# Attention half of a hybrid block: the right half of an output projection by Strassen-Winograd products, with weight sums kept in HBM and a five-slot weight ring

## The reference

```python
def hybrid_layer(x, norm_g, w_in, b_f, conv_w, w_att_o, w_conv_o, w_out):   # x: 256 tokens x 2048
    h = rmsnorm(x, norm_g)
    q, k, v, f_logit, z_att, u, gate_b, gate_c, z_conv, m_att, m_conv = split(h @ w_in)
    o_att = forgetting_attention(heads(q), heads(k), heads(v), log_sigmoid(f_logit + b_f))
    y_att = (o_att * silu(z_att)) @ w_att_o          # 2048 x 2048, the product that the change touches
    o_conv = gate_b * short_conv(gate_c * u, conv_w)
    y_conv = (o_conv * silu(z_conv)) @ w_conv_o
    merged = sigmoid(m_att) * y_att + sigmoid(m_conv) * y_conv
    return x + merged @ w_out                         # then a final rmsnorm
```

## Time and profile before

| | |
|---|---|
| median of 3 runs | 1208.87 us |
| profiled execution, its own time | 1209.7 us |
| its span, first to last instruction | 1207.9 us |
| TensorE busy | 99% |
| VectorE busy | 77% |
| ScalarE busy | 54% |
| HBM traffic | 231 GB/s over the span |

### The profile page before, as it was taken

How to read it: one execution, slowest core, us unless ns; L and a number is a source line. 1 busy time by engine, 2 the same in 40 slices (tenths; PEclk the granted TensorE clock), 3 DMA queues, 4 the chain that set the end, 5 groups by cost and what they waited for, 6 DMA issues and landing times.

```text
span 1207.9 us, 18425 instructions
## 1 busy us (share of the span) xinstructions
PE 1196.3 (99%) x7252; PEld 1070.2 (89%) x7252; DVE 925.3 (77%) x1095; ACT 651.9 (54%) x868; POOL 35.2 (3%) x50
## 2 busy tenths in 40 slices
PE   9999999999999999999999999999999999999997
PEld 8998898898888988889888899999999999888886
DVE  6989988988989989999966556767676667655544
ACT  7666555556656566656555445445544554543533
POOL 1000000000000000000000010111011101000000
PEclk9999999999999999999999999999999999999999
DMA  6788898898888898898678866556655655665663
GB/s 214 240 294 278 270 297 262 274 300 260 272 289 291 270 292 287 270 309 272 192 238 266 269 184 180 155 180 176 188 155 177 181 170 169 223 207 177 212 227 118
DMA packets 181249, 280.40 MB, mean 232 GB/s; under 512 B 9296, under 2 KB 128160, under 8 KB 180768
## 3 DMA queue, kind: packets, MB, share of 16 engines
q1 hardware_dynamic: 171760, 263.49, 68.3%
q10 hardware_dynamic: 9408, 15.78, 4.2%
HBM read 270.83 MB, written 8.41 MB: 231 GB/s over the span
## 4 chain that ended last, share of the span: by engine, by line
PE 87%; DVE 10%; issue 1%; ACT 1%; DMA 0%; ACTq 0%; POOLq 0%; POOL 0%; DVEq 0%
PE ps L1478 22%; PE ps L1480 22%; PE ps L1479 22%; PE ps L1494 7%; PE ps L1493 6%; PE ps L1495 3%; PE ps L1492 3%; DVE w_lo L1052 2%; DVE w_lo L1089 2%; DVE w_lo L1086 2%; DVE quads L1068 1%; DVE quads L1070 1%; DVE quads L1066 1%; DMA chan_rows<-in_norm_gain 0%; PE ps L1503 0%
## 5 line engine op out<-in xcount | busy, mean ns | idle before, releaser
L934 DVE TENSOR_TENSOR w_lo<-w_raw,w_hi 128x1024 fp32r<-128x1024 f32 x196 | 238.8, 1236 | 99.6 <-ACT w_hi L610 98.9
L1478 PE MATMUL ps<-h,w_hi 128*128 128x258 f32 (+1 forms) x1024 | 293.6, 287 | 1.4 <-DVE w_lo L1052 1.2
L1479 PE MATMUL ps<-h,w_hi 128*128 128x258 f32 (+1 forms) x1024 | 291.2, 284 | 0.0
L1480 PE MATMUL ps<-h,w_lo 128*128 128x258 f32 (+1 forms) x1024 | 290.9, 284 | 0.0
L610 ACT CAST w_hi<-w_raw 128x1024 fp32r<-128x1024 f32 x198 | 204.3, 1051 | 120.1 <-PE ps L1480 74.8
L1478 PEld LDWEIGHTS ps<-h,w_hi 128*128 128x128 f32 x1024 | 192.7, 188 | 5.4 <-issue 1.8
L1479 PEld LDWEIGHTS ps<-h,w_hi 128*128 128x128 f32 x1024 | 192.9, 188 | 2.1
L1480 PEld LDWEIGHTS ps<-h,w_lo 128*128 128x128 f32 x1024 | 192.8, 188 | 0.0
L1052 DVE TENSOR_TENSOR w_lo<-w_raw,w_hi 128x1024 fp32r<-128x1024 f32 x122 | 148.7, 1220 | 15.9 <-ACT w_hi L666 15.7
L1494 PE MATMUL ps<-h,w_hi 128*128 128x512 f32 x408 | 159.9, 397 | 1.0 <-DVE w_lo L1052 0.9
L666 ACT CAST w_hi<-w_raw 128x1024 fp32r<-128x1024 f32 x122 | 127.0, 1049 | 29.2 <-PE ps L1480 25.1
(11 more groups left out here) (211 smaller groups left out, 2055.2 us busy)
## 6 DMA issues: line engine op xcount, KB each, us to landing
w_raw<-in_w_in SPq DMA_DIRECT2D x226, 512.0 KB, 4.9
quads<-in_w_in SPq DMA_DIRECT2D x144, 512.0 KB, 4.5
w_raw<-in_w_conv_o SPq DMA_DIRECT2D x32, 512.0 KB, 5.7
w_raw<-in_w_att_o SPq DMA_DIRECT2D x32, 512.0 KB, 4.6
w_raw<-in_w_out SPq DMA_DIRECT2D x32, 512.0 KB, 4.5
quads<-in_w_in SPq DMA_DIRECT2D x48, 256.0 KB, 5.0
gates_dram<-stage ACTq DMA_DIRECT2D x24, 256.0 KB, 4.9
gate_nat<-gates_dram ACTq DMA_DIRECT2D x8, 512.0 KB, 4.1
```

Of the source, the lines that this page charges most:

```text
L934: nc.vector.tensor_tensor(w_lo[:, lo_slot(c), :], w_raw[:, c % RAW, :], w_hi[:, hi_slot(c), :].bitcast(F32), ALU.subtract).then_inc(w_spli ...
L1478: nc.tensor.matmul(dst, a_hi, b_hi, start=start, stop=False, skip_group_check=resumed)
L1479: nc.tensor.matmul(dst, a_hi, b_lo, start=False, stop=False, skip_group_check=resumed)
L1480: return nc.tensor.matmul(dst, a_lo, b_hi, start=False, stop=stop, skip_group_check=resumed)
```

## The change

Columns 0 to 1023 of `w_att_o` are still multiplied by `natural`-like units (two blocks, `"n"`). For columns 1024 to 2047 the product of 256 tokens x 2048 by 2048 x 1024 is cut in 2 x 2 parts (two token halves, even and odd k tiles, two column halves) and made from seven products of half size in place of eight: 56 products instead of 64. The weight sums T1 to T4 are made by VectorE during the pairs of att, from weights loaded for that purpose (`load_t`, 1 MB a pair), and stored to HBM (`store_t`, `t_dram`, 1 MB a pair); the sums of the attention output, S1 to S4, are made in `finish_pair`, split, stored for seven pairs (512 KB each) and brought back in one 3.5 MB transfer on POOL's queue when wa begins. In wa, sums are loaded back as weight units. Such a unit (`"a"`, `"t1"`, `"b"`, `"t2"`, `"b22"`) is 512 KB as well, but gives two products and not four. Wa has 44 units where it had 32:

```diff
 def hi_slot(c):
-    return (c - U_F) % CONV_RING if c < U_F else (c + 5) % RING
+    return (c - U_WIDE) % CONV_RING if c < U_WIDE else (c - U_WIDE + CONV_RING) % RING
 def slot_reused(c):
-    return RING + c - (CONV_RING if c < U_F else RING) + 1
+    return RING + c - (CONV_RING if c < U_WIDE else RING) + 1
...
+        M_TURN = (LEFT_END + 3, RIGHT_END + 4, N_WA + 2, N_WA + 4)
+        M_ROUND = (LEFT_END + 4, RIGHT_END + 5, N_WA + 3, N_WA + 5)
+        GATED = (LEFT_END + 1, RIGHT_END + 1, N_WA, N_WA + 3)
...
+            def beside(n):
+                i, j = divmod(n, N_ATT)
+                if j == 0 and 0 <= i - 1 < PAIRS:
+                    load_t(i - 1)
+                if j == 8 and 0 <= i - 1 < PAIRS:
+                    store_t(i - 1)
+                if j == 7 and 0 <= i - 2 < PAIRS - 1:
+                    store_os(i - 2)
...
+            pool.wait_ge(w_used, RING + U_WA)
+            pool.wait_ge(os_stored, (PAIRS - 1) * 16)
+            nc.gpsimd.dma_start(os[:, 0:PAIRS - 1, :, :, :].rearrange("p i s n t -> p i (s n t)"),
+                                os_dram.rearrange("i p x -> p i x")).then_inc(os_landed, 16)
...
+            def sum_t(i, n):            # VectorE, at j == 7 (n 0, 1) and j == 11 (n 2, 3)
+                ...
+                if n == 0:
+                    dve.wait_ge(t_landed[i % 2], (i // 2 + 1) * 16)
+                    nc.vector.tensor_tensor(t(T3), b12, b22, ALU.add).then_inc(t_summed, 1)
...
             for i in range(PAIRS):
                 for j in range(1, N_ATT + 1):
-                    split_unit(None, 0, U_ATT + i * N_ATT + j + LEAD)
                     if i > 0:
                         finish_pair(i - 1, j)
...
+                    if i > 0 or j > 1:
+                        split_unit(None, 0, U_ATT + i * N_ATT + j + LEAD_5)
...
+            def merge_whole(nb):
+                bank = nat_bank(nb)
+                dve.wait_ge(w_used, RING + U_WA + (LEFT_END, RIGHT_END)[nb] + 1)
+                ...
+                nc.vector.tensor_tensor(merged[:], ps[:, bank:bank + 2, :], gate_wa[:, nb, :, :], ALU.mult
+                                        ).then_inc(free[bank], 1)
+                dve.wait_ge(free[bank], FREE_A["wa"] + 1)
+                add_partial(nb)
+
+            def combine():
+                dve.wait_ge(u_kept, 1)
+                dve.wait_ge(p_kept, 2)
+                ...                     # four adds of 128x512
...
+            for n in range(1, UNITS - U_WA - LEAD_5):      # VectorE, wa and out
+                if n <= 9:
+                    finish_pair(PAIRS - 1, n)
+                if n == A_END + 1:
+                    dve.wait_ge(p_kept, 1)
+                    nc.vector.tensor_tensor(left_c[:, 0, :], left_c[:, 0, :], ps[:, P2_BANK, :], ALU.add
+                                            ).then_inc(c11_summed, 1)
+                if n == N_WA:
+                    combine()
+                for nb, place in enumerate(GATED):
+                    if n == place and nb < 2:
+                        merge_whole(nb)
+                    elif n == place:
+                        merge_products(nb)
+                for nb, place in enumerate(M_ROUND):
+                    if n == place:
+                        split_m(nb)
+                split_unit(None, 0, U_WA + n + LEAD_5)
...
+            def branch_unit(n):         # TensorE, one unit of wa
+                ...
+                pe.wait_ge(w_split, RAW + c + 1)
+                ...
+                elif kind == "a":
+                    product(p1, *o_piece(2 * first, 0), *w(left), **ends(first))
+                    last = product(p2, *o_piece(2 * first + 1, 0), *w(right), **ends(first))
...
+            for n in range(N_WA):
+                branch_unit(n)
+                if n < 4:
+                    finish_pair(PAIRS - 1, n)
+                for nb, place in enumerate(M_TURN):
+                    if n == place:
+                        turn_m(nb)
```

More of the change, by code:

```diff
@@ L81, with wa_order, out_order @@
 N_BRANCH = 2 * KT
+NAT_UNITS = KT // 2
+def wa_order():
+    first, second = [], []
+    for two in range(STEPS // 2):
+        first += [("a", 2 * two), ("a", 2 * two + 1), ("t1", two)]
+        second += [("b", 2 * two), ("b", 2 * two + 1), ("t2", two), ("b22", two)]
+    right = iter([("n", 1, j) for j in range(NAT_UNITS)])
+    found = [("n", 0, j) for j in range(NAT_UNITS)]
+    for n, unit in enumerate(first):
+        found.append(unit)
+        if n % 3 == 2:
+            found.append(next(right))
+    found.append(next(right))
+    for n, unit in enumerate(second):
+        found.append(unit)
+        if n in (2, 4, 6):
+            found.append(next(right))
+    return found
+def out_order():
+    found = []
+    for first, stop in ((0, 8), (8, 12), (12, 16)):
+        found += [(k, c) for c in range(2) for k in range(first, stop)]
+    return found
+WA_ORDER, OUT_ORDER = wa_order(), out_order()
+N_WA = len(WA_ORDER)
+A_END = max(n for n, unit in enumerate(WA_ORDER) if unit[0] in ("a", "t1"))
+LEFT_END = WA_ORDER.index(("n", 0, NAT_UNITS - 1))
+RIGHT_END = WA_ORDER.index(("n", 1, NAT_UNITS - 1))
 U_F = CONV_UNITS + HOSTED
@@ L380, in hybrid_block @@
         q_split = sem("q_split")
+        t_landed, t_stored = ([sem(f"{name}{n}") for n in range(2)] for name in ("t_landed", "t_stored"))
+        t_summed = sem("t_summed")
+        os_made, os_rounded, os_split = sem("os_made"), sem("os_rounded"), sem("os_split")
+        os_stored, os_landed = sem("os_stored"), sem("os_landed")
+        p_kept, c11_summed, u_kept, right_made = sem("p_kept"), sem("c11_summed"), sem("u_kept"), sem("right_made")
         kq_rounded, v_rounded, p_rounded = sem("kq_rounded"), sem("v_rounded"), sem("p_rounded")
@@ L479, in load, with load_t @@
                 sp.dma_start(dst, src).then_inc(w_landed[c % RAW], 16)
[L481 to L490, removed]
+            def load_t(i):
+                if i > 1:
+                    sp.wait_ge(t_stored[i % 2], i // 2 * 16)
+                sp.dma_start(t_quads[:, i % 2, :, :, :], w_att_k[:, 2 * i:2 * i + 2, UNIT:D].rearrange(
+                    "p k (n c) -> p k n c", n=2)).then_inc(t_landed[i % 2], 16)
@@ L536, in _ @@
             load_natural(U_WC, w_conv_k)
[L537 to L542, removed]
+            for n in range(N_ATT * PAIRS):
+                i, j = divmod(n, N_ATT)
+                rows = slice(j % PER * UK, j % PER * UK + UK)
+                col = (COL_K, COL_Q, COL_V)[j // PER] + i * 2 * P
+                load(None, 0, U_ATT + n, w_in_k[:, rows, col:col + 2 * P])
+                beside(n)
+            for n in range(N_WA):
+                load_wa(n)
+                beside(N_ATT * PAIRS + n)
+            for n, (k, c) in enumerate(OUT_ORDER):
+                load(None, 0, U_OUT + n, w_out_k[:, k:k + 1, c * UNIT:(c + 1) * UNIT], k=1)
             sp.wait_ge(w_used, RING + U_OUT)
@@ L783, in _, with load_gate, make_gate @@
             act.dma_start(neg_c_dram, neg_c[:]).then_inc(c_stored, 16)
[L786 to L795, removed]
+            def load_gate(which, nb, dst):
+                act.dma_start(dst, gates[which].rearrange("(t p) n -> p t n", p=P)[:, :, nat_cols(nb)]
                               ).then_inc(gate_landed, 16)
-            def make_gate(which, nb):
+            def make_gate(which, nb, dst):
                 act.wait_ge(gate_landed, (which * NB + nb + 1) * 16)
-                nc.scalar.activation(gate_nat[:], gate_nat[:], ACT.Sigmoid).then_inc(gate_made, 1)
+                nc.scalar.activation(dst, dst, ACT.Sigmoid).then_inc(gate_made, 1)
             for nb in range(NB):
@@ L1342, in split_m, with add_partial @@
                                         ALU.subtract).then_inc(m_split, 1)
[L1344 to L1350, removed]
+            def add_partial(nb):
+                nc.vector.tensor_tensor(merged[:], merged[:], partial[:, :, nat_cols(nb)], ALU.add
+                                        ).then_inc(merged_made, 1)
@@ L1358, in _ @@
[L1358 to L1366 removed]
+                else:
+                    dve.wait_ge(os_made, 4 * PAIRS)
+                nc.vector.tensor_tensor(merged[:], ps[:, bank:bank + 2, :], gate_wa[:, nb, :, :], ALU.mult
+                                        ).then_inc(free[bank], 1)
```

283 lines of the change are left out of this document (215 added, 68 removed).

## The result

The changed kernel takes 1216.12 us (median of four runs, 1215.52 to 1217.15); the kernel before, on the same chip, 1208.87. The ratio is 1.0061, 95% interval 1.0044 to 1.0079: slower by 0.6%. The profiled execution takes 1215.55 us, 5.85 more than the one before. The forecast was 1211.7: the right direction, but 4.4 us short, and the measured time lies only 0.5 us inside the upper end of the range (1216.6).

The account below looks back on a forecast made before the run. TensorE's own instructions were taken to bound the kernel. -5.5 (matmuls), +4.8 (late units) and +3.5 (turn) gave +2.8 on 1209.7, so 1212.5; the median, 0.8 lower, was forecast at 1211.7 us, range 1204.8 to 1216.6.

Parts of the forecast that it names:

- The removed matmuls: In wa, 24 matmuls fewer at 0.2275 us each save 5.5 us, the bound of the gain.
- Att, wc and the five slots at nothing: VectorE's and DMA's added work in att, and the five-slot ring with its new order in wc and att, cost 0.
- The round trip: In wa, four units can't come faster than landing plus 2.6 us; taken as 7.8 us, seven trips from unit 15 to 43.
- the term of 4.8: Late unit supply in wa makes unit 43 start 4.8 us late, of which a merge adds 1.3.
- The transfer at nothing: POOL's 3.7 MB load at wa's start, beside the weight units, adds 0 to the sum.
- late sums at unit 10: Rival: stored sums arrive late, TensorE stands at unit 10 for 3 to 6 us more, 1214.7 to 1217.7; chance 0.08.
- the margin of 2.5 us: In wa, unit 15 is split at 9.2 us, TensorE reaches it at 11.7, counted from its start on unit 8.
- four split and four loading units hide most: At 305 GB/s some 7 us of DMA work remain at unit 10 of wa, mostly hidden by units held ready or loading.
- The rule that was weighed there: DMA engines serve queues in turn: half of 394 GB/s each, 3.7 MB in 19 us and a unit in 2.7 us.
- The turn before block 2: TensorE waits 3.5 us there, because combine stands behind unit 47's split and block 2 is merged late.
- the forecast's +2.8: Net change on the profiled execution: -5.5 for removed matmuls, +4.8 for late units, +3.5 for the turn.
- The clock: Rival: the 3.5 us idle before the turn drops TensorE's clock, next unit 2.7 us slower, 1214.4 us; chance 0.07.

Follow-up runs that it names:

- eight buffers and the split transfer: Changed kernel with eight raw weight buffers for units 11 to 43 of wa and the stored-sums transfer cut into four parts: 1207.52 us, ratio 0.9983.
- the kernel without the transfer: Changed kernel without POOL's 3.7 MB transfer; seven pairs' products take the output itself, so numbers differ from the reference: 1213.47 us, ratio 1.0036.
- the kernel with eight buffers: Changed kernel with eight raw weight buffers in place of four for units 11 to 43 of wa, stored-sums transfer left whole: 1209.03 us, ratio 0.9994.
- half loads: Changed kernel where two-product units load only 256 KB of 512 KB, same compute, numbers not the reference's: 1207.20 us, ratio 0.9979.
- split transfer: Changed kernel, still four raw buffers, with the stored-sums transfer cut into four DMAs started after units 0, 3, 6 and 9: 1215.12 us, ratio 1.0044.

## Why the prediction came out right, and 4.4 us short

**The removed matmuls: right.** The first to the last matmul of wa and out take 181.46 us before and 177.53 with eight buffers and the split transfer. That is 3.9 less, and 5.46 is the bound. Of the 1.5 between them 0.6 is a gap before TensorE at the `o` wait, and some 0.5 is the slower pace of the products with `os`, which the prediction priced like all others; the rest is spread over many rows.

**Att, wc and the five slots at nothing: right.** Wa begins at 1018.96 where it began at 1019.13, after 96 units with two more kinds of work beside them. VectorE's share there became 76%, where 78% was worked out. One wait of 0.4 us stands in att, where the prediction had none.

**The round trip: right.** Seven of them were to take 55.9 us with the merge, and took 56.4; landing plus 2.6 gives 5.4 + 2.6 = 8.0. With the transfer gone the term of 4.8 (the delay at unit 43) measured 4.9. Fewer bytes a load or one more buffer removes it.

**The transfer at nothing: the step that failed.** The prediction priced 3.7 MB beside the units at 0 ("In the sum 0") and held late sums at unit 10 to be the only harm (3 to 6 us, 0.08). TensorE did wait there, 1.3 us. The cost came by another way: the seven units loaded beside the transfer landed after 11.2 us, unit 15 was split about 4 us later than worked out, the margin of 2.5 us at that unit was gone, and a loop that is slower than TensorE never gives such a delay back. By the forecast's own sum, 13.2 (split 15 after unit 8's due start, for 9.2) + 56.4 - 60.3 = 9.3 at unit 43, where it had 4.8. With unit 44 the term measured 10.5, about 5.0 of it the transfer's (97.54 against 92.06, less the 0.5 of the operand). The arithmetic that hid it was "four split and four loading units hide most". That cover exists, but it is the same cover that the next stretch was to live on, and it was counted twice.

The rule that was weighed there can be judged now. The transfer took 22.2 us for 3.67 MB, 165 GB/s, and seven units came in about the same time, of a total of 369 GB/s in 1022 to 1045 us. The Trainium skill (DMA: Bandwidth & Descriptors, Queues, rings and completion order), that an engine takes packets from its queues in turn, agrees with these equal shares, and so does the kernel with eight buffers: more loads were waiting beside the transfer, and it still landed after 21.2 us. What the prediction made of the rule was off: half of 394 GB/s gives a unit in 2.7 us only if nothing else moves, and here one came in 3.5 us.

**The turn before block 2: mis-sized.** 3.5 us forecast, 0.7 measured from start to start (0.6 in the list of waits; all of out is 1.0 longer). `combine` follows the split of unit 47, which ended 6.3 us after unit 43's start and not 7.8, since four splits stood ready in a row; and TensorE itself came to the turn 1.2 us later than worked out, 0.9 of it a wait at unit 44. So the two errors have opposite signs: +5.7 on the supply (10.5 for 4.8), -2.5 on the turn (1.0 for 3.5), in sum 3.2 over the forecast's +2.8, which makes the 6.0. The remaining 1.4 us is the median: forecast 0.8 below the profiled execution, it lies 0.6 above this one. That the time still fell inside the range is partly luck: had the turn cost its 3.5 us, the median would have been some 2.5 us higher and outside. The time also lies in the band of the rival with the late sums (1214.7 to 1217.7), but not by that rival's way.

**The clock: a rival that did not come, with a price that was half right.** The changed kernel's longest idle stretch in wa and out is 1.5 us and its clock stayed at 1.00 there. Where a variant stood idle for 2.7 us the clock fell and cost 1.6 us, against the 2.7 forecast for a whole unit at half speed; it recovered within 4 us. The Trainium skill (TensorE: Matmul & The Clock Gate, HAM oscillation) warns of such gaps between bursts, and the trace of the kernel without the transfer agrees: 0.57 after the gap, 1.00 before it.

**Left open.** Whether the order of loads in the transfer's first 20 us could hide it wholly was not tried; neither was the idle time at which the clock falls.

## What to carry to other kernels

A change that halves the work for each loaded unit halves the time that the loader has. Before making it, divide landing plus rounding plus splitting by the number of raw buffers and compare with the time the bound engine takes for a unit, on the average over a stretch that is longer than the units held ready: 8.0 / 4 = 2.0 against 1.74 cost some 5 us in wa, 8.0 / 5 = 1.6 let TensorE run through wa without a wait. And a large transfer issued at a stage's start is not free because nobody waits for it: its price is the delay of the loads beside it, and when the stage behind it can't catch up that delay stays to the end.

## What was not expected of the hardware

With 391 GB/s moving in 1030 to 1040 us, loads of 512 KB landed after 11.2 us at the median and up to 13.5, where they need 4.8 with 214 GB/s. Idle stretches of 1.7 us (half loads) and 1.9 us (eight buffers, whole transfer) left TensorE's granted clock at 1.00. Stretches of 2.06 us (split transfer, shortly after another wait) and 2.7 us (no transfer) were followed by readings of 0.51 over 3 us and 0.57 over 4 us. The 1.9 and the 2.06 differ by 0.2 us and by the wait before, and no run tells which of them counted. With eight buffers and the whole transfer, three of SP's issues of loads between 1036 and 1049 us took 2.4, 4.2 and 3.5 us, where most take 0.4; in the kernels with five or six buffers none in the first 60 us of wa took over 0.8.
